# A ring of weight slots in which the convolutions' units stand 32 bytes further in

## What is computed

```python
u = rms_norm(h, ln_pre_mix[i])
proj = u @ w_in[i]                        # 1024 x 9232
q_a, k_a, v_a, qkv_b, z_b, b_b, a_b, gate_a, gate_b = jnp.split(proj, IN_SPLITS, axis=-1)
...
qkv_b = jax.nn.silu(causal_depthwise_conv(qkv_b, conv_w[i]))     # qkv_b: 256 x 3072
```

## Time and profile before

| | |
|---|---|
| Median of three runs | 988.51 us |
| The profiled execution | 988.56 us |
| Its span, first to last instruction | 986.8 us |
| TensorE matmuls busy | 969.2 us, 98% |
| TensorE weight loads busy | 827.6 us, 84% |
| VectorE, ScalarE, GpSimd busy | 365.4, 512.0, 742.0 us |
| Mean granted TensorE clock | 0.997 |
| From HBM | 165.32 MB, 169 GB/s over the span |

### The profile page before, as it was taken

The page is one execution under the profiler, slowest core; times in us unless marked ns, Lnnn a source line. Parts: engine busy times, 40 slices in busy tenths (PEclk is TensorE's granted clock), DMA queues, the critical chain, the costliest instruction groups (busy, mean ns, idle before and its releaser), DMA issues.

```text
span 986.8 us, 15319 instructions
## 1 busy us (share of the span) xinstructions
PE 969.2 (98%) x6004; PEld 827.6 (84%) x6004; DVE 365.4 (37%) x841; ACT 512.0 (52%) x758; POOL 742.0 (75%) x592
## 2 busy tenths in 40 slices
PE   6999999999999999999999999999999999999997
PEld 6988889988888888888898887899888888888885
DVE  4687524776524235112111345243252251111103
ACT  5576624465624446555434546585466474444431
POOL 6967633877642998899977887868877789888890
PEclk9999999999999999999999999999999999999998
DMA  7646332545332766667655566655655457666541
GB/s 260 208 131 191 103 112 60 176 151 171 96 120 60 256 216 200 217 198 213 190 156 185 160 206 214 214 163 166 197 175 168 144 170 219 190 186 186 185 129 43
DMA packets 76752, 167.37 MB, mean 170 GB/s; under 512 B 8348, under 2 KB 13704, under 8 KB 76552
## 3 DMA queue, kind: packets, MB, share of 16 engines
q1 hardware_dynamic: 71296, 156.40, 51.6%
q10 hardware_dynamic: 5384, 9.99, 3.1%
HBM read 165.32 MB, written 1.05 MB: 169 GB/s over the span
## 4 chain that ended last, share of the span: by engine, by line
PE 97%; DVE 2%; ACT 1%; DMA 0%; issue 0%; DVEq 0%
PE L L513 22%; PE L L515 22%; PE L L514 22%; PE Q L513 2%; PE Q L515 2%; PE Q L514 2%; PE L L870 2%; PE L L871 2%; PE L L872 2%; PE Q L1070 1%; PE Q L730 1%; PE Q L1052 1%; PE Q L1150 1%; PE L L784 1%; PE L L786 1%; PE L L785 1%
## 5 line engine op out<-in xcount | busy, mean ns | idle before, releaser
L503 POOL TENSOR_TENSOR w_lo<-raw,w_hi 128x512 fp32r<-128x512 f32 x588 | 741.8, 1303 | 219.2 <-ACT w_hi L1293 218.6
L1293 ACT CAST w_hi<-raw 128x1024 fp32r<-128x1024 f32 x294 | 305.3, 1054 | 245.4 <-PE L L515 108.0
L513 PE MATMUL L<-w_hi,uH 128*128 128x512 f32 (+1 forms) x768 | 304.4, 396 | 0.3
L515 PE MATMUL L<-w_hi,uL 128*128 128x512 f32 (+1 forms) x768 | 296.5, 386 | 0.0
L514 PE MATMUL L<-w_lo,uH 128*128 128x512 f32 (+1 forms) x768 | 295.8, 385 | 0.0
L513 PEld LDWEIGHTS L<-w_hi,uH 128*128 128x128 f32 x768 | 144.4, 188 | 30.0 <-DVE uL L1908 1.5
L515 PEld LDWEIGHTS L<-w_hi,uL 128*128 128x128 f32 x768 | 144.3, 188 | 29.8
L514 PEld LDWEIGHTS L<-w_lo,uH 128*128 128x128 f32 x768 | 144.6, 188 | 27.1 <-issue 0.5
L513 PE MATMUL L<-w_hi,hH 128*128 128x512 f32 x176 | 69.0, 392 | 0.0
L515 PE MATMUL L<-w_hi,hL 128*128 128x512 f32 x176 | 68.6, 390 | 0.0
L514 PE MATMUL L<-w_lo,hH 128*128 128x512 f32 x176 | 68.5, 389 | 0.0
(11 more groups left out here) (352 smaller groups left out, 1313.4 us busy)
## 6 DMA issues: line engine op xcount, KB each, us to landing
raw<-in_w_in SPq DMA_DIRECT2D x88, 512.0 KB, 3.7
raw<-in_w_ffn_gate SPq DMA_DIRECT2D x22, 512.0 KB, 3.7
raw<-in_w_ffn_up SPq DMA_DIRECT2D x22, 512.0 KB, 3.6
raw<-in_w_ffn_down SPq DMA_DIRECT2D x22, 512.0 KB, 3.5
raw<-in_w_gate SPq DMA_DIRECT2D x22, 512.0 KB, 3.8
raw<-in_w_up SPq DMA_DIRECT2D x22, 512.0 KB, 3.7
raw<-in_w_down SPq DMA_DIRECT2D x22, 512.0 KB, 3.5
raw<-in_w_out SPq DMA_DIRECT2D x16, 512.0 KB, 4.2
```

Source lines behind the costliest of these rows:

```text
L503: last = nc.gpsimd.tensor_tensor(lo[:, cc], raw[:, n % RAW, cc], hi[:, cc].bitcast(F32), ALU.subtract)
L513: mm(dst, sH, wH, start=start, stop=False)
L515: return mm(dst, sL, wH, start=False, stop=stop)
L1293: copy(halves[SLOT[u]][0], raw[:, u % RAW, :]).then_inc(w_hi_there, 1)
```

## The change

A unit of a convolution stands 8 floats (32 bytes) into its slot, all others at its beginning. So a convolution's unit reaches 32 bytes into the slot behind it, and the two tensors become 128 floats longer. Two rules are added to `BEFORE`: a convolution's unit also waits for the last unit of the next slot if that one is not shifted, and a unit that isn't shifted waits for the last unit of the slot ahead of it if that one is. Behind them all tensors move up: `w_lo` by 512 bytes, `uH` and all that follow by 1024.

```diff
+    def lead(n):
+        return 8 if UNITS[n][0][0] == "conv" else 0
+
...
-        BEFORE.append(newest.get(slot, -1))
+        others = [newest.get(slot, -1)]
+        if slot < SPLIT:
+            others += [m for m in [newest.get(slot + 1, -1)] if m >= 0 and slot + 1 < SPLIT and lead(n) and not lead(m)]
+            others += [m for m in [newest.get(slot - 1, -1)] if m >= 0 and not lead(n) and lead(m)]
+        BEFORE.append(max(others))
...
-        w_hi = place("w_hi", [P, SPLIT, UNIT], F32R)
-        w_lo = place("w_lo", [P, SPLIT, UNIT], F32R)
+        w_hi = place("w_hi", [P, SPLIT * UNIT + P], F32R)
+        w_lo = place("w_lo", [P, SPLIT * UNIT + P], F32R)
...
+        def halves(n):
+            if SLOT[n] >= SPLIT:
+                return extra[SLOT[n]]
+            at_ = slice(SLOT[n] * UNIT + lead(n), (SLOT[n] + 1) * UNIT + lead(n))
+            return w_hi[:, at_], w_lo[:, at_]
```

More of the change, by code:

```diff
@@ L356, in build @@
         lent = {SPLIT: (84, 88), SPLIT + 1: (92, 96), SPLIT + 2: (68, 72), SPLIT + 3: (76, 80), SPLIT + 4: (60, 64), SPLIT + 5: (-8, -4)}
-        halves = {n: (w_hi[:, n, :], w_lo[:, n, :]) for n in range(SPLIT)}
-        for n, (hi_at, lo_at) in lent.items():
-            halves[n] = (big(f"w_hi{n}", hi_at, [P, UNIT], F32R)[:], big(f"w_lo{n}", lo_at, [P, UNIT], F32R)[:])
+        extra = {n: (big(f"w_hi{n}", hi_at, [P, UNIT], F32R)[:], big(f"w_lo{n}", lo_at, [P, UNIT], F32R)[:]) for n, (hi_at, lo_at) in lent.items()}
+        def halves(n):
[3 more added lines that the diff above has]
+            return w_hi[:, at_], w_lo[:, at_]
         used = B + 100 * KB
@@ L501, in _ @@
                     cc = slice(half * UNIT // 2, (half + 1) * UNIT // 2)
-                    hi, lo = halves[SLOT[n]]
+                    hi, lo = halves(n)
                     last = nc.gpsimd.tensor_tensor(lo[:, cc], raw[:, n % RAW, cc], hi[:, cc].bitcast(F32), ALU.subtract)
@@ L1292, in split_up_to @@
                         act.wait_ge(*VE(("dnorm",), "da", 2 * GH - 1))
-                    copy(halves[SLOT[u]][0], raw[:, u % RAW, :]).then_inc(w_hi_there, 1)
+                    copy(halves(u)[0], raw[:, u % RAW, :]).then_inc(w_hi_there, 1)
                     made[0] += 1
```

## The result

The kernel after takes 992.02 us (median of six runs, 991.65 to 992.43) where six runs of the kernel before, made beside them, took 988.51 (988.25 to 988.94): ratio 1.0033, 95% interval 1.0023 to 1.0043. The forecast was 988.2. The time lies within 0.8 us of rival A's 991.2, but two of its terms were not A's, as will be seen.

The account below looks back on a forecast made before the run. TensorE, holding 97% of the chain of waits, was taken to bound the kernel. Terms of -3.84 (rhythm), +0.8 (taken back), +2.7 (wait) and 0 (rest) gave -0.3 us, a median of 988.2 us, range 985.5 to 992.4.

Parts of the forecast that it names:

- rival A: Convolutions and `scan 0`: rhythm independent of address, only the wait acts, 0 + 2.7 us, 991.2 us; chance 0.28.
- Part 1: Convolutions' 576 matmuls: the 32-byte shift brings starts from 120 to 113.3 ns apart, -3.84 us.
- the run at 231 ns: 512-column matmuls after a pause: ten steps in 2.31 us, read as showing that the surplus goes in steps.
- rival C: Convolutions: a smaller gain, 117 ns between two steps, -1.6 + 0.2 + 2.7 us, 989.8 us; chance 0.08.
- Part 2: First convolution group and steps behind it: TensorE waits for GpSimd, VectorE and ScalarE, taking back 0.8 us.
- Part 3: `scan 0`: unit 40's copy waits for unit 35, 3.21 us later, delaying `vn` copies; TensorE idles, +2.7 us.
- Part 4: Everything else: 512-column matmuls keep their rhythm despite moved tensors, and no clock fall in the pause; 0 us.
- The sum: Whole kernel: -3.84 + 0.8 + 2.7 = -0.3 us, median becoming 988.2 us.
- The rest of Part 4: 512-column matmuls with `w_lo` and `uH` moved: steady rhythm of 226.7 ns kept, 0 us; worst bound 231 ns.

Follow-up runs that it names:

- experiment 3: The kernel after, with ScalarE copying unit 40 behind its work in `scan 0`, shift and waits kept: 988.15 us, ratio 0.9993 to the kernel before.
- experiment 4: The kernel after, with convolution units 64 bytes into their slots in place of 32, waits included: 988.67 us, ratio 1.0001 to the kernel before.
- experiment 1: The kernel after, with convolution units back at their slots' beginnings, added waits and longer tensors kept: 992.82 us, ratio 1.0036 to the kernel before.
- experiment 7: The kernel after, with tensors behind the ring 64 bytes further, convolution units 128 bytes in, unit 40 copied late: 998.64 us, ratio 1.0099 to the kernel before.
- experiment 2: The kernel after, with slots 4160 bytes apart, the 32-byte shift kept and the old `BEFORE`: 996.08 us, ratio 1.0070 to the kernel before.
- experiment 6: The kernel after, with convolution units 64 bytes in and unit 40 copied behind ScalarE's `scan 0` work: 987.08 us, ratio 0.9980 to the kernel before.

## Why the prediction was wrong, by its own steps

**Part 1 failed, above all in one sentence of it:** "if the pattern repeats each 64 bytes, a shift by 32 puts the weight load half a period off". That the rhythm hangs on the address was right (experiments 3 and 4, against rival A's root). The size of the step, 6.7 ns, turned up too, 113.4 ns in experiment 4, and no mean distance came under 113.3; but it did so at 64 bytes, where by the same sentence nothing should have changed, so the agreement with the forecast's 113.3 is no support for its reason. The period was read from the `ba` pieces, which are 16 columns wide, 64 bytes long; that they all run alike says that a load of 64 bytes is short, and not that a load of 512 bytes sees the same thing each 64. The second support, that the surplus "goes in steps", was weak as well: the run at 231 ns is a mean of single distances between 224 and 236 ns, and what 32 bytes gave is such a mix, too. At 32 bytes the matmuls got 1.65 ns each and not 6.67: -0.95 us, where the term said -3.84. On this side rival C (117 ns) came nearest, with a chance of 0.08. Why the rhythm is better at 64 bytes and hardly at 32 stays open.

The rule of the Trainium skill, "TensorE: Matmul & The Clock Gate", section "Step-by-step: what each phase is for", that moving columns and weight load have independent read ports, had been weighed as speaking for no effect. The runs do not bear out a rhythm without effect of the addresses: 120.0 ns (experiment 1), 118.3 (the change) and 113.4 (experiment 4) with one operand moved by 0, 32 and 64 bytes in three kernels that differ in nothing else. Whether one of the two takes bandwidth from the other is not shown by that.

**Part 2** took back 0.8 us of a gain of 3.84, which was too much, though both places were right. Where the gain came, in experiment 4, 0.25 us is taken back around L969, most of it where TensorE waits for ScalarE. The 0.2 us of waiting for GpSimd did not come there, because the clock's late rise had put TensorE behind; it stands in experiment 7, whose clock rose early. At a gain of 0.95 there was little to take back: the traces of the change and of experiment 3 lose 0.1 us at L969.

**Part 3 was right** in place, cause and size. Forecast: the cast of unit 40 3.21 us later, 2.7 us idle ahead of L1102 (now L1115), no further delay from the order. Measured: an idle wait of 3.24 us on ScalarE, 2.66 us more between L1111 and L1115, 2.76 up to `conv 1, 0`, and nothing at units 36 to 39: experiment 3 keeps their waits and has no loss.

**Part 4 named the clock and priced it at nothing.** "The granted clock stood through all shorter pauses; should it fall in the 2.7 us pause, some microseconds more are lost. I take 0." It fell in two of the three traces of the change and of its waits alone, for 1.6 us, and by the mean granted clock in nine of eleven runs of the change, so the medians (992.0, 992.2) have it. No row of the kernel before could show it, since it has no such pause there. Such a term, which no row bounds at zero, should have stood in the sum with part of its price, and among the rivals with a chance of its own.

**The sum** was -3.84 + 0.8 + 2.7 + 0 = -0.3. The runs have -0.95 + 0.1 + 2.76 + 1.6 = +3.5, and 3.5 was measured; the address side was off by 2.2 us and the clock side by 1.6, both the same way. The steps that failed are these two: the period in Part 1 and the clock put at nothing in Part 4. Rival A (0 + 2.7) came close to the time because its two errors, the small gain and the lost clock, have opposite signs. The time lies inside the range of 985.5 to 992.4, but only near its end.

**The rest of Part 4** held, by the reason it gave. The 512-column matmuls kept their rhythm (227.6 ns in the mean, 227.7 before), with `uH` moved by 1024 bytes and `w_lo` by 512, both multiples of 512. Experiments 2 and 7 show what a move by 64 would have cost: 9 to 14 us. I had bounded it by 231 ns, and 232 to 233 is where it goes.

## What to carry to other kernels

Where a slot's rule of reuse is tightened, find the copy that now waits and read what stands behind it in the same engine's program: a copy whose unit was not used for another 20 us cost 2.8 us, because a result that TensorE wanted was queued behind it, and moving the copy behind that result brought all of it back. A gain in single distances is worth following matmul by matmul against the trace before, since that tells what a neighbour takes back from what the clock does at the start. An idle stretch of a busy TensorE of some microseconds should be priced with what the clock may take after it (here 2.5 us idle, 1.6 us more). And the places of stationary and moving operand to one another are worth a measurement in a TensorE-bound fp32r kernel, each matmul shape by itself, since the same 64 bytes gave up to 3.8 us on the one and took 14 from the other.

## What the runs showed of the hardware

- The distance of two fp32r matmuls of 256 columns, each with its load of 128 columns, is 120.0 ns where both operands stand at the same place modulo 512 bytes, 118.3 at 32 bytes, and 113.4 at 64. With 512 columns it is 226.7 ns in a steady run at 0, some 229 in the mean at 256, and 232 to 233 at 64, 320 and 384 (experiments 2 and 7).
- The rhythm at 113.4 ns is a state that a run of matmuls gets into or not: the same addresses gave 113.4 in one trace and 118 in another for the second group of convolutions (experiments 4 and 6), and within experiment 7 one step of six has 117.8 and the others 113 to 114. It was also seen at 320 bytes with the roles exchanged (experiment 2). 113.4 and 120.0 are regular; what lies between is a mix of single distances.
- After 2.50 us in which TensorE did nothing its granted clock was 0.50 for 3.4 us in three of five traces, beginning 0.9 us after it had started again in two of them (idle until 162.41, lower from 163.27; 162.76 and 163.68) and at once in the third (162.13 and 162.17).
- The clock's rise at the start of the kernel came at 12.0 to 14.7 us in different executions of much the same program, which moves a single run by some 1.3 us (half of 2.7 us).
